# Input projections of two layers taken from the unscaled residual, with the norm's factor applied where the banks are read

## What is computed

```python
def rmsnorm(x, w):
    xf = x.astype(jnp.float32)
    y = xf * lax.rsqrt(jnp.mean(xf * xf, axis=-1, keepdims=True) + EPS)
    return (y * w.astype(jnp.float32)).astype(x.dtype)
...
    for l in range(DEPTH):
        h = rmsnorm(x, attn_norm_w[l])
        proj = h @ w_in[l]
        (z, xbc, dt_raw, sc_b, sc_c, sc_h, q, k_c, v_c, k_s, v_s, k_w, v_w,
         g_nsa) = jnp.split(proj, split_at, axis=-1)
        y_ssd = ssd_mixer(z, xbc, dt_raw, ...)
        y_sc = sc_b * causal_dwconv(sc_c * sc_h, sc_conv_w[l])
        y_nsa = nsa_mixer(q, k_c, v_c, k_s, v_s, k_w, v_w, g_nsa, cos, sin, ...)
        x = x + jnp.concatenate([y_ssd, y_sc, y_nsa], axis=-1) @ w_out[l]
        h = rmsnorm(x, ffn_norm_w[l])
        ...
```

## Time and profile before

| | us |
|---|---|
| median of 3 runs (lowest, highest) | 2299.12 (2298.26, 2299.53) |
| the profiled execution | 2300.56 |
| its span | 2298.8 |
| PE busy in the span | 2275.1 |
| DVE busy in the span | 1689.1 |
| ACT busy in the span | 946.6 |
| mean granted TensorE clock | 0.998 of full speed |

### The profile page before, as it was taken

One profiled execution on the slowest core, in us unless ns is written; L12 is line 12 of the kernel. 1 busy time (PEld: TensorE's weight loads), 2 busy tenths in 40 slices (PEclk: granted clock), 3 DMA queues, 4 the chain that ended last, 5 costly groups with the idle time before them and its releaser, 6 DMA issues.

```text
span 2298.8 us, 35341 instructions
## 1 busy us (share of the span) xinstructions
PE 2275.1 (99%) x14452; PEld 2020.6 (88%) x14452; DVE 1689.1 (73%) x2780; ACT 946.6 (41%) x1413; POOL 116.1 (5%) x77
## 2 busy tenths in 40 slices
PE   9999999999999999999999999999999999999998
PEld 9899999899998888898779888888888888989997
DVE  6889878889889858855455983884885673797774
ACT  5866545766542122235554221223321222475443
POOL 0010010110100000010001000001000001001001
PEclk9999999999999999999999999999999999999999
DMA  7345465354545535532121553553454352303543
GB/s 267 143 166 184 165 232 224 116 202 178 187 149 210 186 136 193 190 112 91 37 74 56 192 193 118 172 179 126 150 196 158 138 178 100 137 36 147 184 156 119
DMA packets 66881, 355.08 MB, mean 154 GB/s; under 512 B 7328, under 2 KB 10528, under 8 KB 42912
## 3 DMA queue, kind: packets, MB, share of 16 engines
q1 hardware_dynamic: 65888, 352.23, 43.2%
q10 hardware_dynamic: 832, 0.59, 0.1%
HBM read 351.75 MB, written 1.05 MB: 153 GB/s over the span
## 4 chain that ended last, share of the span: by engine, by line
PE 91%; DVE 6%; ACT 1%; issue 1%; DMA 0%; ACTq 0%; DVEq 0%
PE bank L532 90%; DVE sb_w_lo L2210 2%; ACT sb_w_hi L1448 1%; PE bank L1400 1%; DVE sb_products L2244 1%; PE bank L1274 0%; DMA sb_consts<-consts 0%; DVE sb_nP L2896 0%; DVE sb_nP L2869 0%; DVE sb_latP L3029 0%; DVE sb_decays L2908 0%; ACT sb_decays L1448 0%; DVE sb_mid L2968 0%; ACT sb_nP L1448 0%; DVE sb_normed L3166 0%
## 5 line engine op out<-in xcount | busy, mean ns | idle before, releaser
L2210 DVE TENSOR_TENSOR sb_w_lo<-sb_raw,sb_w_hi 128x2048 fp32r<-128x2048 f32 (+3 forms) x280 | 564.1, 2015 | 124.7 <-ACT sb_w_hi L1448 121.5
L1448 ACT ACTIVATE sb_w_hi<-sb_raw 128x2048 fp32r<-128x2048 f32 (+5 forms) x301 | 491.4, 1634 | 382.5 <-PE bank L532 382.2
L532 PE MATMUL bank<-sb_f_pair,sb_w_hi 128*128 128x256 f32 (+1 forms) x2090 | 523.9, 339 | 5.2 <-DVE sb_w_lo L2210 4.2
L532 PE MATMUL bank<-sb_h_hi,sb_w_hi 128*128 128x512 f32 (+1 forms) x1400 | 510.9, 365 | 0.7 <-DVE sb_w_lo L2210 0.4
L532 PE MATMUL bank<-sb_h_lo,sb_w_hi 128*128 128x512 f32 (+1 forms) x1400 | 507.3, 362 | 0.0
L532 PE MATMUL bank<-sb_h_hi,sb_w_lo 128*128 128x512 f32 (+1 forms) x1400 | 507.2, 362 | 0.0
L532 PEld LDWEIGHTS bank<-sb_f_pair,sb_w_hi 128*128 128x128 f32 x2090 | 360.4, 190 | 51.9 <-DVE sb_w_lo L2210 7.2
L2244 DVE CUSTOM_DVE_ANT_0 sb_products<-sb_raw,sb_cond,sb_params 128x1024 f32<-128x1024 f32 x280 | 360.1, 1286 | 32.5 <-DVEq L2246 15.8
L532 PE MATMUL bank<-sb_f_pair,sb_w_lo 128*128 128x256 f32 (+1 forms) x1122 | 366.1, 326 | 0.0
L532 PEld LDWEIGHTS bank<-sb_h_hi,sb_w_hi 128*128 128x128 f32 x1400 | 264.2, 189 | 42.7 <-issue 0.9
L532 PEld LDWEIGHTS bank<-sb_h_lo,sb_w_hi 128*128 128x128 f32 x1400 | 264.2, 189 | 41.5 <-issue 0.5
(11 more groups left out here) (317 smaller groups left out, 2919.3 us busy)
## 6 DMA issues: line engine op xcount, KB each, us to landing
sb_raw<-w_mod SPq DMA_DIRECT2D x144, 512.0 KB, 3.2
sb_raw<-w_l_up SPq DMA_DIRECT2D x44, 1024.0 KB, 4.8
sb_raw<-w_l_in SPq DMA_DIRECT2D x22, 1024.0 KB, 6.1
sb_raw<-w_l_down SPq DMA_DIRECT2D x32, 704.0 KB, 4.4
sb_raw<-w_m0a_up SPq DMA_DIRECT2D x22, 1024.0 KB, 4.8
sb_raw<-w_m0b_up SPq DMA_DIRECT2D x22, 1024.0 KB, 4.8
sb_raw<-w_m1a_up SPq DMA_DIRECT2D x22, 1024.0 KB, 4.8
sb_raw<-w_m1b_up SPq DMA_DIRECT2D x22, 1024.0 KB, 4.8
```

Of the source, the lines that this page charges most:

```text
L532: return nc.tensor.matmul(out, lhsT, rhs, start=start, stop=stop, skip_group_check=True)
L1448: return nc.scalar.activation(out, in_, func, **kw)
L2210: V.tensor_tensor(split_part(*at, w_lo[s]), landed_part(*at, raw[raw_slot(*at)]), split_part(*at, w_hi[s]).bitcast(F32), ALU.subtract).the ...
```

## The change

The input tiles are made of the residual times the gain alone, without the norm's factor: in layer 0 as soon as a tile of x has landed (DVE makes both parts, L2310's place is taken by `first_input`), in layer 1 beside the last panels of `l0_down` (ACT the high part, DVE the low part in `second_input`). The sums for the norm go to the middle of panel 1 and the spreading of the factor behind two steps of panel 2; the factor is kept in SBUF (`rstd_of`) by DVE. It is applied where a bank is left: by ACT's `evacuate(0)`, by DVE's new `scale_in(j)` for the panels 3 to 9 and 11, by the rotation tables (`turning`) and by the copies of v. Panel 9 takes the square of the factor, and panel 10 none. In DVE's order `dt_soft` stands ahead of `in_low(3)`, and the condition tiles stand beside the panels 2 to 4. The modulation pieces stay at their panels. SP issues x before the weights, the first panel in two parts, and the parameters and constants two panels later.

```diff
@@ SP
-            for q in (0, 2):
+            for q in (0, 2, 3):
...
-                if (name, n) == ("l0_in", 1):
+                if (name, n) == ("l0_in", IN_ORDER[3]):
                     sp.dma_start(params[:, KD:PARAM_W], ...
-                if (name, n) == ("l0_in", IN_ORDER[2]):
+                if (name, n) == ("l0_in", IN_ORDER[4]):
                     sp.dma_start(consts[:, P:CONST_W], ...
...
+                begin = FRONT_HALVES[0][1] if k == 0 else 0
+                if begin:
+                    sp.dma_start(raw[slot][:, 0:begin], src[:, 0:begin]).then_inc(S("front_landed"), 16)
@@ PE
                     if t == 0:
+                        if l == 0:
+                            first_sums()
+                        else:
+                            token_sums()
                         panel(L + "_in", IN_ORDER[1])
...
+                def taken(i):
+                    if 3 <= i < 10 or i == 11:
+                        pe.wait_ge(S("in_scaled"), q + (i - 2 if i < 10 else 8))
+                    else:
+                        pe.wait_ge(S("in_evac"), e + min(i, 9) + 1)
...
-                in_steps(32, 56)
+                in_steps(32, 34)
+                if l == 0:
+                    pe.wait_ge(S("ident_in"), 16)
+                spread_rstd(l)
+                in_steps(34, 42)
+                spread_condition(0)
+                in_steps(42, 50)
+                spread_condition(1)
+                in_steps(50, 56)
...
-            keep_clock(10)
...
+            keep_clock(18)
             for l in range(LAYERS):
                 mixers(l)
...
-                if l < LAYERS - 1:
-                    norm_by_token(l + 1, 1)
@@ ACT
+                root_by_token(take("norm_sum", 0))
...
+                    if 3 <= j < 9:
+                        act.wait_ge(S("in_scaled"), q + j - 2)
+                    else:
+                        panel_done(L + "_in", n)
                     if j == 0:
+                        act.wait_ge(S("rstd_ready"), l + 1)
                         for tb in range(2):
-                            last = run(tm[:, tb, :], bank[2 + tb][:, 0:TM], ACT.Copy)
+                            last = run(tm[:, tb, :], bank[2 + tb][:, 0:TM], ACT.Identity, scale=rstd[:, tb:tb + 1])
...
+                    elif j in (7, 8):
+                        last = run(u, u, ACT.Silu)
...
+                ahead(0)
+                evacuate(0)
+                act.wait_ge(S("dt_raw"), l + 1)
                 (the three exponentials)
+                evacuate(1)
+                ahead(1)
+                condition(0)
+                evacuate(2)
+                ahead(2)
+                condition(1)
+                ahead(3)
+                evacuate(3)
...
-                evacuate(9)
                 ssd_gap(3)
@@ DVE
+            def raw_low(l, k):
+                V.scalar_tensor_tensor(h_thin[1][:, k, :], res[:, k, 0:T], par(f"attn_norm{l}", k, k + 1),
+                                       h_thin[0][:, k, :].bitcast(F32), ALU.mult, ALU.subtract).then_inc(S("norm_split"), 1)
+            def first_input():
+                dve.wait_ge(S("gain_in"), 16)
+                for n in range(KD + 1):
+                    if n < KD:
+                        dve.wait_ge(S(f"x_in{n // 2}"), 16)
+                        V.tensor_scalar(h_thin[0][:, n, :], res[:, n, 0:T], par("attn_norm0", n, n + 1), None,
+                                        ALU.mult).then_inc(S("first_high"), 1)
+                    if n:
+                        dve.wait_ge(S("first_high"), n)
+                        raw_low(0, n - 1)
+                front_low("l0_in", 0)
+                front_low("l0_in", 1)
+                dve.wait_ge(S("first_sq"), KD)
+                for n in (4, 2, 1):
+                    out = first_squares[:, 0:n, :]
+                    link(V.tensor_tensor(out, out, first_squares[:, n:2 * n, :], ALU.add))
+                dve.sem_inc(S("first_added"), 1)
...
+                def spread_in():
+                    dve.wait_ge(S("rstd_spread"), l + 1)
+                    V.tensor_copy(rstd_of, rstd_spread).then_inc(S("rstd_kept"), 1)
+                    dve.wait_ge(S("rstd_kept"), l + 1)
+                    V.tensor_tensor(rstd_squared, rstd_of, rstd_of, ALU.mult)
+                def scale_in(j):
+                    n = IN_ORDER[j]
+                    panel_done(f"l{l}_in", n)
+                    x = (rstd_squared if j == 9 else rstd_of).unsqueeze(1).to_broadcast([P, 2, T])
+                    V.tensor_tensor(U[:, 2 * n - 2:2 * n, PAD:UW], in_bank(j)[:, :].rearrange("p (a t) -> p a t", a=2), x,
+                                    ALU.mult).then_inc(S("in_scaled"), 1)
...
+                if l:
+                    mod_part("l1_in", IN_ORDER[0], 0)
+                else:
+                    dve.wait_ge(S("params_in"), 16)
+                    dve.wait_ge(S("ident_in"), 16)
+                    conditions(0, 8)
+                in_low(2)
                 dt_biased()
-                in_low(2)
+                spread_in()
                 if l:
                     mod_part("l1_in", IN_ORDER[0], 1)
+                else:
+                    conditions(8, 12)
+                dt_soft()
                 in_low(3)
-                dt_soft()
                 if l:
                     mod_part("l1_in", IN_ORDER[1], 0)
                     mod_part("l1_in", IN_ORDER[1], 1)
+                else:
+                    conditions(12, 16)
+                turning()
                 in_low(4)
-                keys()
+                rs, xs = keys()
+                scale_in(3)
                 in_low(5)
+                key_tiles(rs, xs)
+                scale_in(4)
                 queries()
+                in_low(6)
                 conv(0)
-                in_low(6)
                 conv(1)
+                scale_in(5)
+                in_low(7)
                 conv(2)
                 conv(3)
...
-                if l == 0:
-                    conditions(0, 4)
-                in_low(7)
-                if l == 0:
-                    conditions(4, 8)
                 conv(4)
+                scale_in(6)
                 conv(5)
+                in_low(8)
...
                 conv(6)
                 conv(7)
+                scale_in(7)
...
+                in_low(9)
                 maxes(0)
-                in_low(9)
+                scale_in(8)
...
                 mats(3)
+                scale_in(9)
                 out(2)
...
                 probs(3)
+                scale_in(11)
                 low(f"l{l}_out", 0)
```

More of the change, by code:

```diff
@@ L873, in mixers @@
                 h = h_thin
[L875 to L880, removed]
-                if l == 0:
[L882 to L895, removed]
-                        if k == KD // 2:
-                            panel(L + "_in", 0)
-                        for tb in range(2):
-                            last = mm(bank[2 + tb][:, 0:T], h[0][:, k, tb * P:(tb + 1) * P],
-                                      front_low[:, k * TM:k * TM + T], False, k == KD - 1)
-                else:
-                    w = panel(L + "_in", 0)
-                    for k in range(KD):
-                        ready(k)
-                        for tb in range(2):
-                            last = mm3(bank[2 + tb][:, 0:T], both(h, slice(None), k, slice(tb * P, (tb + 1) * P)),
-                                       cols(w, k * TM, T), k == 0, k == KD - 1)
@@ new lines, in mixers @@
+                e = take("in_evac", 10)
+                q = take("in_scaled", 8)
+                front_high, front_low = w_hi[half_slot(L + "_in", 0)], w_lo[half_slot(L + "_in", 0)]
+                if l:
+                    pe.wait_ge(S("high"), SPLIT_AT[L + "_in", 0] + 1)
+                for k in range(KD):
+                    if l == 0 and k < KD - 2:
+                        pe.wait_ge(S("front_high"), k // 2 + 1)
+                    elif l == 0:
+                        pe.wait_ge(S("high"), 1)
+                    ready(k)
+                    for tb in range(2):
+                        o, x = bank[2 + tb][:, 0:T], both(h, slice(None), k, slice(tb * P, (tb + 1) * P))
+                        mm(o, x[0], front_high[:, k * TM:k * TM + T], k == 0, False)
+                        mm(o, x[1], front_high[:, k * TM:k * TM + T], False, False)
@@ L908, in mixers @@
+                for k in range(KD):
+                    if l == 0 and k == 0:
+                        pe.wait_ge(S("front_low"), 1)
+                    if k == (0 if l else KD // 2):
+                        panel(L + "_in", 0)
+                    for tb in range(2):
+                        last = mm(bank[2 + tb][:, 0:T], h[0][:, k, tb * P:(tb + 1) * P],
+                                  front_low[:, k * TM:k * TM + T], False, k == KD - 1)
                 last.then_inc(S("panels_used"), 1)
@@ L1844, in mixers @@
                     high("l0_in", 1)
-                else:
```

(14 more changed lines are left out.)

221 lines of the change are left out of this document (94 added, 127 removed).

## The result

The changed kernel takes **2312.62 us** (median of 5 runs, 2310.13 to 2317.15) against 2299.12 for the kernel before beside it (2298.26 to 2303.25). The ratio is 1.0058 (95% interval 1.0047 to 1.0070), 0.6% slower. The forecast was 2305.5 with a range up to 2309.0: right in direction, 7.1 us too small. The profiled execution took 2312.62 us with a span of 2310.8, 12.0 us longer than the 2298.8 of before.

The account below looks back on a forecast made before the run. PE was taken to bound the kernel, busy 2275 of 2298.8 us. Layer 0 adds 1.75, layer 1 3.1 and the clock 1.5, together 6.35 us: profiled 2306.9, median 2305.5, range 2297.5 to 2309.

Parts of the forecast that it names:

- Layer 0, entry: Start of layer 0: unscaled tiles let products begin near 7 and panel 2 at 20.5, 5.5 us earlier.
- P2: The time at which panel 2 starts on PE: forecast 20.5 in layer 0, 348.5 in layer 1.
- Panel 3, layer 0: PE idles 4.85 us for DVE's low part behind condition tiles and softplus; start 32.45, net 0.25 us earlier than before.
- P3: The time at which panel 3 starts on PE: forecast 32.45 in layer 0, 358.0 in layer 1.
- Layer 1, entry: Start of layer 1: panel 2 3.3 us earlier, then 3.3 us idle before panel 3; net 0.1 us later.
- The tails: End of the mixers, where DVE's added factors come late: 2.0 us lost in layer 0, 3.0 in layer 1.
- The clock: Half clock behind the two new panel 3 waits: 1.5 us for the longer, 0 for the shorter.
- the first case: Kernel before, near 11.2 to 14.5: granted clock fell to half after PE idled 0.91 us amid filling and tiny products.
- Both waits lose the clock: Rival: both panel 3 waits are paid in clock too, 2307.0 us; chance 0.15.
- No difference: Rival: panel 3 waits come but the tails don't, 2299 to 2301 us, 2303 with half the tails; chance 0.32.
- the early start doesn't come: Rival: weights' first half or gain lands at 8 us or later, panel 2 some 2 us later, 2307.5; chance 0.05.
- Faster, if panel 3 is not held up: Rival: panel 3's low part is ready in time, giving back 9.65 us, 2296 or even 2294 or less; chance 0.15.

Follow-up runs that it names:

- low3_first: Changed kernel with panel 3's low part put back ahead of the condition tiles and softplus; 2302.24 us, ratio 1.0014.
- filled_fit: Changed kernel plus idle PE products cut to fit the waits (20, 14 and four times 5), nothing else moved; 2306.40 us, ratio 1.0027.
- best_x: Changed kernel with DVE's order improved at panel 3 and in the tails, plus all four input-tile pairs on one queue; time not given in the text, nothing gained.
- before_delayed: Kernel before plus three repeated group-score products on DVE, lengthening the first head pair's wait in both layers; 2304.16 us, ratio 1.0016.

## Why the prediction was right or wrong

- **Layer 0, entry.** P2 was forecast at 20.5 and came at 21.76. The first product came at 9.07, not 7.1: ACT's copy of the front half waited for its 350 KB until 8.48, where I had taken 6.6 for the landing. The gain landed in time (3.5 us from issue). DVE also lost 1.17 us to the second pair of x and was done with low part 2 at about 21.7, so both were last together.
- **Panel 3, layer 0.** Right: P3 is P2 + 12.18 (forecast 11.95), idle 4.87 (4.85), by the chain named. `low3_first` shows that this order is the cause.
- **Layer 1, entry.** Right. Taking off the 5.82 us that layer 0 brings along, P2 is at 348.9 (348.5) and P3 at 358.8 (358.0), so P2 + 9.9 (9.5), idle 3.44 (3.3).
- **The tails.** Their waits were named rightly: `scale_in(8)` ahead of ACT (0.9 later in layer 1, forecast 1.0), `scale_in(9)` ahead of panel 10, `scale_in(11)` ahead of the reciprocal (0.84, forecast 0.65). In layer 0 the stretch from the transposes (77.42, now 81.17) to the head rstd grew by 2.07, forecast 2.0, but that is luck: 0.7 of it is the fall behind the first head pair, and with the clock full (`filled_fit`) it grew by 1.37. In layer 1 it grew by 4.83 against 3.0, and the difference is the clock's: with the clock full and the 0.66 taken off, layer 1 as a whole adds 3.2 to layer 0, forecast 3.1. Layer 0 adds 2.7, forecast 1.75. There two errors work against each other: panel 3 starts 1.5 us later than forecast in the changed kernel (33.94 against 32.45) and 1.8 later in `filled_fit`, and the tail costs 0.6 less.
- **The clock: the step that failed.** "I take 1.5 for the longer one, nearest to the first case, and 0 for the shorter one." Measured: 7.7 us. Three errors made it. The longer wait drew a fall of two units (3.4 us), not one; the shorter one drew one (1.7); and the tails' waits of 1.3 to 1.5 us, which follow from my own terms (0.65 before plus 0.65), drew three more in layer 1 and one in layer 0. Of these 12.0 us of lost clock 7.7 reached the time. I had priced only the two long ones, because the trace of before has nothing between the 1.02 us that cost nothing and these. The sum without the clock, 4.85, stands against 5.9 measured in the two layers. With 7.7 in place of 1.5 it gives 12.6, against 13.6 in the two layers and 13.5 between the medians. By the profiled executions alone the miss looks smaller, 5.7 us (2306.9 against 2312.62); the profiled execution of the kernel before was 1.44 above its median, and that of the changed kernel was its median.
- **The rule weighed there** (the Trainium skill, TensorE: Matmul & The Clock Gate, "What's actually happening": slow is the default state, activity releases it) pointed the right way and to a higher price for both long waits. The traces agree as far as these two go: falls follow the waits of 4.87 and 3.44 us in both profiles of the changed kernel. They add that waits of 1.24 to 1.50 us are enough at some places and not at others.
- **The rivals.** "Both waits lose the clock", 2307, was the nearest, still without the tails' falls. "No difference" fell with the tails. The condition of "the early start doesn't come" was half met: the front half of the weights was there only at about 8.4, but the first product still came 4.7 us earlier than before and panel 2 was 1.26 us later than forecast, not 2. "Faster, if panel 3 is not held up" had the right switch: `low3_first` turned it and won 10.4 us, forecast 9.65.

## What to carry to other kernels

When an edit lengthens waits of the engine that bounds the kernel, price each new wait twice, for its length and for what the granted clock does behind it; here waits up to 1.02 us in dense work drew no fall and some from 1.24 us on did, and the clock was 7.7 of the 13.6 us lost. Before an instruction is moved ahead in a full queue, ask when its own input is ready and what stands behind it: the softplus, moved ahead in the kernel before, kept DVE idle for 5.32 us until its exponentials came, and the condition tiles of the changed kernel kept it idle for 2.85. If the waits can't go, a few idle products in them can keep the clock full, if they end with the wait.

## What the runs showed of the hardware that was not expected

- Falls of the granted clock behind waits come in units: in every profile each lasted 3.4 us at half speed (1.7 us of work lost) or two or three times that (3.4 us lost behind waits of 4.87 and 2.14 us and behind one of the two of 4.66, 5.1 behind one of 2.26).
- Whether a wait draws one is not settled by its length. Waits of 1.27, 1.31, 1.40, 1.41, 1.49, 1.64 (`best_x`, ahead of panel 2) and 1.78 us drew none in one place or run; 1.24 (`best_x`, head pair 0), 1.25, 1.31, 1.41, 1.44 and 1.50 did in another. Up to 1.02 us none was seen in dense work. The changed kernel's two profiles agreed place for place, while the ten runs of `before_delayed` spread over 6.5 us with mean clocks of 0.996 to 0.999. What decides it was not tried.
- A fall costs less than its 1.7 us where the engine would have waited next anyway: about 0.7 at the head pairs of both layers.
